# Moving residuals, turns and last convolutions of a fused four-layer kernel across its pair and layer changes

## What is computed

```python
# L0: window attention, L1: state-space mixer (x, z, B, C, dt from ssm_w_in)
h_lat = layer_norm(ALPHA * h_lat + g_m_l * y_lat, ln_mix_g[i], ln_mix_b[i])
f_lat = squared_relu_mlp(modulate(h_lat, sh_f_l, sc_f_l), ff_w1[i], ff_w2[i])
h_lat = layer_norm(ALPHA * h_lat + g_f_l * f_lat, ln_ff_g[i], ln_ff_b[i])
...
# L2: gated linear attention and Fourier mix, L3: attention; both then:
def conv_ffn(h, w_up, w_conv, b_conv, w_down):
    u = dwconv_centred(h @ w_up, w_conv, b_conv)
    g, v = jnp.split(u, 2, axis=-1)
    return (jax.nn.silu(g) * v) @ w_down
```

## Time and profile before

| what | value |
| --- | --- |
| median of 3 runs | 4105.22 us (4103.78, 4105.22, 4110.1) |
| profiled execution | 4101.45 us, span 4099.5 us |
| mean granted TensorE clock | 0.986 of full |
| TensorE busy (PE) | 3906.3 us, 95% of the span |
| DVE, ACT, POOL busy | 2190.2, 838.8, 575.1 us |

### The profile page before, as it was taken

The page is one execution under the profiler, slowest core; times in us unless marked ns, Lnnn a source line. Parts: engine busy times, 40 slices in busy tenths (PEclk is TensorE's granted clock), DMA queues, the critical chain, the costliest instruction groups (busy, mean ns, idle before and its releaser), DMA issues.

```text
span 4099.5 us, 47553 instructions
## 1 busy us (share of the span) xinstructions
PE 3906.3 (95%) x18322; PEld 2437.5 (59%) x18322; DVE 2190.2 (53%) x3633; ACT 838.8 (20%) x1655; POOL 575.1 (14%) x936
## 2 busy tenths in 40 slices
PE   7999999999999999999999998899999999999998
PEld 6677588844455555558744646645555444758863
DVE  0254532356667566444556016737788555538876
ACT  1166111100112312212101113521100012531000
POOL 1000000033313422400132002200001320000012
PEclk9999999999999999999999998999999999999999
DMA  5256011245412222312344212501112541002234
GB/s 186 92 187 207 21 52 62 83 165 173 137 63 93 79 84 85 106 59 93 124 165 144 72 41 84 182 25 62 52 62 72 173 166 55 22 22 83 92 124 158
DMA packets 209773, 410.69 MB, mean 100 GB/s; under 512 B 5922, under 2 KB 92280, under 8 KB 209424
## 3 DMA queue, kind: packets, MB, share of 16 engines
q1 hardware_dynamic: 203696, 386.94, 27.8%
q0 software_dynamic: 5856, 20.73, 1.6%
HBM read 405.49 MB, written 2.16 MB: 99 GB/s over the span
## 4 chain that ended last, share of the span: by engine, by line
PE 86%; DVE 7%; ACT 3%; DMA 2%; issue 1%; POOL 0%; DVEq 0%; ACTq 0%; SPq 0%
PE PS L1136 25%; PE PS L1254 18%; PE PS L1096 5%; PE PS L1069 3%; PE PS L1744 3%; PE PS L1047 3%; PE PS L1190 3%; PE PS L1758 3%; PE PS L1006 2%; PE PS L898 2%; PE PS L1745 1%; PE PS L1905 1%; PE PS L1915 1%; PE PS L1380 1%; PE PS L1349 1%
## 5 line engine op out<-in xcount | busy, mean ns | idle before, releaser
L1136 PE MATMUL PS<-UT,RING 128*128 128x256 f32 (+1 forms) x2432 | 640.0, 411 | 10.2 <-ACT BIG L2925 9.1
L1136 PEld LDWEIGHTS PS<-UT,RING 128*128 128x128 f32 x2432 | 461.5, 190 | 151.0 <-issue 14.2
L1136 PE MATMUL PS<-BIG,RING 128*128 128x256 f32 (+1 forms) x1824 | 487.7, 410 | 0.8 <-DVE BIG L2770 0.5
L1136 PEld LDWEIGHTS PS<-BIG,RING 128*128 128x128 f32 x1824 | 345.9, 190 | 106.5 <-DVEq L1981 1.5
L1254 PE MATMUL PS<-RING,BIG 128*128 128x512 f32 x810 | 376.7, 594 | 4.3 <-ACT GATE L2961 2.4
L3540 POOL TENSOR_TENSOR GATE<-BIG 128x128 f32<-128x128 f32 x68 | 33.8, 497 | 1707.5 <-DVE BIG L2776 583.3
L2631 DVE TENSOR_TENSOR RING<-RING 128x512 f32<-128x512 f32 x135 | 108.7, 805 | 297.9 <-DMA RING<-ff_w_dram 176.0
L1254 PEld LDWEIGHTS PS<-RING,BIG 128*128 128x128 f32 x810 | 152.0, 191 | 186.1 <-issue 181.6
L1254 PE MATMUL PS<-RING,RES_TMP 128*128 128x512 f32 x536 | 247.2, 604 | 16.1 <-DVE RING L2634 12.8
L1254 PE MATMUL PS<-RING,GATE 128*128 128x512 f32 x544 | 248.6, 600 | 9.6 <-DVE UT L2663 4.4
L1254 PEld LDWEIGHTS PS<-RING,RES_TMP 128*128 128x128 f32 x536 | 103.0, 193 | 148.3 <-issue 126.0
(11 more groups left out here) (457 smaller groups left out, 5986.1 us busy)
## 6 DMA issues: line engine op xcount, KB each, us to landing
RING<-ff_w_dram SPq DMA_DIRECT2D x112, 1024.0 KB, 5.0
RING<-w_mod_dram SPq DMA_DIRECT2D x48, 2048.0 KB, 8.1
RING<-w_ffn_down_dram SPq DMA_DIRECT2D x55, 1024.0 KB, 4.9
RING<-w_ffn_up_dram SPq DMA_DIRECT2D x44, 1024.0 KB, 5.1
RING<-ssm_w_in_dram SPq DMA_DIRECT2D x8, 2048.0 KB, 8.0
RING<-ssm_w_out_dram SPq DMA_DIRECT2D x4, 2048.0 KB, 7.8
RING<-w_even_in_dram SPq DMA_DIRECT2D x4, 2048.0 KB, 8.0
RING<-att_w_in_dram SPq DMA_DIRECT2D x3, 2048.0 KB, 11.7
```

The costliest lines, as they stand in the source:

```text
L1136: m = mm(bank(bank_, n), a[:, k, :], b[:, k, :], start=k == 0, stop=k == 3)
```

## The change

Seven edits, all of order; no arithmetic is added or dropped.

1. `combined` no longer runs `added(q, 0, 0)` between takes 1 and 2. It moves to DVE's work of slot 1 of the next pair (in L2 and L3 together with `added(q, 0, 1)`, and the others move up). Each take waits for its own product by place.
2. In the last slot of the last pair of each layer the products go in the order P1, P6, P2, P5, P3, P7, P4.
3. The half turns hooked at slots 7 to 10 (L2) and 11 to 14 (L1) of a pair move one slot earlier.
4. `mixer1`, g = 0: C's weights are loaded and used before B's, C's ring half is given back at once, and tile 5 is turned directly behind tile 4.
5. `mixer2`: the turns of tiles 2 and 3 are hooked one place earlier.
6. From L2 to L3: ACT's copy of the turned tile 5 comes only before the key/value copy of tile 2 of `mixer3`.
7. L2 and L3: the convolutions of the last two channel groups move into DVE's work of slots 2 and 4 of down; POOL sums the tokens of slots 2 to 5 before it waits for the hidden values.

```diff
-                    at = {0: 8, 1: 11, 2: 7}[L]
+                    at = {0: 8, 1: 10, 2: 6}[L]
...
+        DOWN_ORDER = ["P1", "P2", "P3", "P7", "P5", "P6", "P4"]
+        DOWN_END = ["P1", "P6", "P2", "P5", "P3", "P7", "P4"]
...
-                           {(0, 0): lambda: outputs_taken(1), (2, 0): lambda: turn_tokens(2, "m", 2), (2, 1): lambda: turn_tokens(2, "m", 3)})
+                           {(0, 0): lambda: outputs_taken(1), (1, 1): lambda: turn_tokens(2, "m", 2), (2, 0): lambda: turn_tokens(2, "m", 3)})
...
                     take(V.tensor_tensor(y1, y2, b("P2"), ALU.add))
-                    early()
-                    dve.wait_ge(S("down_products_done"), 5 * g + 5)
+                    dve.wait_ge(S("down_products_done"), 5 * g + down_place(L, q, "P6"))
                     take(V.tensor_tensor(y2, y2, b("P6"), ALU.add))
+                    dve.wait_ge(S("down_products_done"), 5 * g + down_place(L, q, "P5"))
                     take(V.tensor_tensor(y4, y2, b("P5"), ALU.add))
...
                     if L == 0:
-                        return {2: [partial(added, q, 0, 1)], 3: [partial(added, q, 1, 0)], 4: [partial(added, q, 1, 1)],
+                        return {1: [partial(added, q, 0, 0)], 2: [partial(added, q, 0, 1)], 3: [partial(added, q, 1, 0)], 4: [partial(added, q, 1, 1)],
...
+                if L >= 2:
+                    work[0, 2], work[0, 4] = [partial(last_channels, 0)], [all_channels]
...
-                    if L >= 2:
+                    if L >= 2 and p + 1 < PAIRS[L]:
                         convolved(p, 0)
-                if L < 2:
-                    return
-                convolved(PAIRS[L] - 1, 1)
-                post("hidden_ready")
-                post("conv_vectors_used")
+                return partial(convolved, PAIRS[L] - 1)
...
-                            else:
+                            elif N != 3 or t == a:
                                 turned_tokens(N, "m", t, 4 if N == 1 else 6)
...
+                    if (t, c0) == (2, 1024):
+                        turned_tokens(3, "m", 5)
...
-                        for c0, n in ((b0, 128), (b0 + 512, 128), (SSM_DI + g * 512, 512), (g * 512, 512)):
+                        for c0, n in ((b0 + 512 * (g == 0), 128), (b0 + 512 * (g > 0), 128), (SSM_DI + g * 512, 512), (g * 512, 512)):
...
                         turn_tokens(1, "m", 4, b=4)
+                        turn_tokens(1, "m", 5, b=4)
                         pe.wait_ge(S("ssm_vectors_in"), 112)
                         place(dt)
                         steps_of(0, LAT)
-                        turn_tokens(1, "m", 5, b=4)
```

More of the change, by code:

```diff
@@ L273, in down_banks, with down_order, down_place @@
                     2: dict(P1=0, P2=2, P3=3, P7=6, P5=1, P6=5, P4=4), 3: dict(P1=0, P2=1, P3=4, P7=6, P5=5, P6=3, P4=2)}[L]
+        DOWN_ORDER = ["P1", "P2", "P3", "P7", "P5", "P6", "P4"]
+        DOWN_END = ["P1", "P6", "P2", "P5", "P3", "P7", "P4"]
+        def down_order(L, q):
+            return DOWN_END if q == tiles_of(L)[0] // 2 - 1 else DOWN_ORDER
+        def down_place(L, q, name):
+            return [p for p in down_order(L, q) if p not in ("P3", "P4")].index(name) + 1
         def down_blocks(t):
@@ L1254, in product @@
                             return mm(bank(banks[name]), a, b, start=s == 0, stop=last)
-                        def done(m):
-                            if last:
-                                m.then_inc(S("down_products_done"), 1)
                         weights(t)
                         pe.wait_ge(S("down_tokens_summed"), down_tokens_summed(L, i))
-                        done(product("P1", a11, b11))
-                        done(product("P2", a12, b21))
-                        used(product("P3", s4, b22))
-                        pe.wait_ge(S("down_weights_summed"), down_weights_summed(L, i))
-                        done(product("P7", s3, t3))
-                        done(product("P5", s1, t1))
-                        done(product("P6", s2, t2))
-                        product("P4", a22, t4).then_inc(S("down_slots_done"), 1)
+                        operands = {"P1": (a11, b11), "P2": (a12, b21), "P3": (s4, b22), "P7": (s3, t3), "P5": (s1, t1), "P6": (s2, t2), "P4": (a22, t4)}
+                        summed = False
+                        for name in down_order(L, q) if last else DOWN_ORDER:
+                            if name in ("P7", "P5", "P6", "P4") and not summed:
+                                pe.wait_ge(S("down_weights_summed"), down_weights_summed(L, i))
+                                summed = True
+                            m = product(name, *operands[name])
+                            if name == "P3":
+                                used(m)
+                            elif name == "P4":
+                                m.then_inc(S("down_slots_done"), 1)
+                            elif last:
+                                m.then_inc(S("down_products_done"), 1)
                         if (q, s) in hooks:
@@ L1708, in mixer1 @@
                     else:
-                        wb = ring(weights(t0), 8, 128)
+                        xb, xc = place(cv) * 1024, place(cv) * 1024
+                        wc = ring(weights(t0), 8, 128)
+                        pe.wait_ge(S("down_products_taken"), 7 * (tiles_of(0)[0] // 2 - 1) + 1)
+                        seen(1, "m", 3)
+                        for k in range(KD):
+                            m = mm(PS[:, xc:xc + LAT], wc[:, k, :], UT[:, k, 0:LAT], start=k == 0, stop=k == KD - 1)
+                        used(m)
+                        wb = ring(weights(t0 + 1), 8, 128)
                         outputs_begun(0)
-                        xb = place(cv) * 1024
-                        seen(1, "m", 3)
                         for k in range(KD):
@@ L1715, in mixer1 @@
                         outputs_taken(0)
-                        wc = ring(weights(t0 + 1), 8, 128)
-                        x = place(cv) * 1024
-                        for k in range(KD):
-                            mm(PS[:, x:x + LAT], wc[:, k, :], UT[:, k, 0:LAT], start=k == 0, stop=k == KD - 1)
                         turn_tokens(1, "m", 4, b=4)
+                        turn_tokens(1, "m", 5, b=4)
                         pe.wait_ge(S("ssm_vectors_in"), 112)
@@ L1727, in mixer1 @@
                             mb = mm(PS[:, xb + 512:xb + 512 + CTX], wb[:, k, :], UT[:, k, LAT:TOK], start=k == 0, stop=k == KD - 1)
-                        mb.then_inc(wused, 2)
+                        used(mb)
                         start_of_steps()
@@ L2479, in mixer1 @@
                     for n in range(6):
-                        ready(cv, t0 + n if n < 2 else t0 + 2 if n == 5 else None)
+                        ready(cv, t0 + (n if g else 1) if n < 2 else t0 + 2 if n == 5 else None)
                         x = n % 4 * 1024
@@ L2648, in take, with combined @@
                     dve.wait_ge(S("down_products_taken"), taken["n"])
-                def combined(q, early):
+                def combined(q):
                     g = g0 + q
@@ L2815, in _ @@
                 residual(L, flow(L, "mixed", ntok), T0[L, "out"], n)
-                paired_up(L)
+                last_channels = paired_up(L)
                 if L == 0:
                     offer(flow(1, "conv", 4))
-                paired_down(L)
+                paired_down(L, last_channels)
                 post("layer_done")
@@ L3631, in _ @@
                 if L in next_of:
+                    ahead = 2 if L < 2 else 6
+                    sums_of_down_tokens(L, range(2, ahead))
                     pool.wait_ge(S("hidden_ready"), nth(L))
@@ L3634, in _ @@
                     behind = 14 if L < 2 else 10
-                    sums_of_down_tokens(L, range(2, behind))
+                    sums_of_down_tokens(L, range(ahead, behind))
                     store_gates(next_of[L])
```

15 lines of the change are left out of this document (10 added, 5 removed).

## The result

The changed kernel takes 4057.5 us (median of 4 runs, 4056.13 to 4061.04), the kernel before 4106.18 us on the same chip (its three runs and a fourth): ratio 0.9882, 95% interval 0.9865 to 0.9899. Its profiled execution took 4056.13 us, span 4054.1 us, 45.4 us less than before, at a mean granted clock of 0.991 (0.987 to 0.991 in its four runs). The median lies where it was forecast; in the sum behind it one term is 3.1 us too large, one is right as a whole and wrong in both its parts, and the stretches that the change doesn't touch moved by up to 1.9 us one way and 3.2 us the other.

The account below looks back on a forecast made before the run. TensorE was taken to bound the kernel, with gains only in its idles and low clock: 35.3 us idle plus 12.4 us clock, 47.7 off 4101.45, gives 4053.8; the median, 3.77 above, 4057.5 us, range 4047 to 4076.

Parts of the forecast that it names:

- The take chain: Pair changes: without the residual between takes and the turn ahead of P1's copy, 15.6 us idle and 3.6 us clock gained.
- The last convolutions: Down stage of L2 and L3: waits of 5.15 and 2.41 us go, 7.9 us with tails, plus 2.65 us clock.
- Start of L3: L3's first products: earlier start and a shorter wait behind ACT's and DVE's work, 4.8 us idle, 2.6 us clock.
- End: End of the kernel: one residual fewer between the last takes and the last norm, about 0.4 us gained.
- Start of L2: L2's start: earlier turn hides ACT's 3.04 us copy but for about 0.5; net 2.3 us idle, 1.8 us clock.
- Rival D: Pair changes: waits only change names, P3 waiting for something else that ends at the same time; 4100 to 4108 us, chance 0.02.
- Start of L1: L1's mixer: x's weights land earlier, so its products start 4.3 us sooner; 1.6 and 0.2 us of clock at x.
- Rival B: Whole kernel: clock loss moves elsewhere or stays, little of 12.4 us comes back; 4067 to 4070 us, chance 0.2.

Follow-up runs that it names:

- The control: The changed kernel, unaltered, on another chip: 4055.38 us against 4098.6 us for the kernel before there, ratio 0.9891.

## Why the prediction was right, and where it was off

- *The take chain* (15.6 us and 3.6 of clock): the six changes gained 19.2 us in the first profile (4.2 + 2.1 + 2.3 + 1.8 + 7.0 + 1.9, rounded). Undone, they cost 14.9 us with L2's turn still in its new slot. What I missed is that the same residual alone would have cost 5.2 us at L1's start; only edit 2 makes that small.
- *The last convolutions* (7.9 us and 2.65): 8.5 + 2.7 = 11.2 us, and 9.5 when undone. The cover was judged too large: "less 3.32 us of idle it makes them 1.0 us late, under the 3.75 us of slack" holds in the middle of a pair, and not at a stage's start, where 1.3 us was left. The term held because this was still above nothing.
- *Start of L3* (4.8 and 2.6 us): 7.5 measured. *End* (0.4): 0.5.
- *Start of L2* (2.3 and 1.8): 3.7 measured, and near the 4.1 forecast only by luck. "The turn one place earlier hides the second but for about 0.5" failed: 2.69 us of 3.04 stayed, so that the idle fell by 0.3 us (5.13 to 4.78) and not by 2.3. The first wait didn't grow either. The other 3.4 us are clock, 1.7 behind each of two waits of before, where I had counted one. Rival D, on one place: the wait changed its name. Whether edit 5 is worth anything is open, since no run undoes it alone.
- *Start of L1*: the term that was mis-sized as a whole. Its idle came out: 5.03 us (0.94 + 3.13 + 0.96) of the 9.16 in the trace before, 4.1 us gained for a forecast 4.3. Its clock didn't. I had the 1.8 us of low clock behind the 5.73 us wait come back, and they did. But a wait of 3.13 us took the place of the one of 3.04, and this one has low clock behind it, 0.9 us on the turn and 2.0 us on the steps, where the old one had none: 3.0 us in all, not 6.1. Rival B, on one place.
- *What no term had*: 1.1 us ahead of the first change, 0.7, 1.9 and -3.2 us in stretches that the change leaves alone, 0.5 us together. The 1.9 us are clock that the kernel before happened to lose: 0.95 of full was granted there from 3650 to 3686 us, and 1.00 in the changed kernel. In the fourteen profiles the stretch up to the linear attention's row took 470.1 to 474.7 us and the attention of L3 229.1 to 232.6.
- *The median* was hit by luck. The profiled execution took 4056.13 us where 4053.8 was forecast, 2.3 us too much; and the median lies 1.4 us above it, not 3.77 as before. The two nearly cancel. The control gave 43.2 us of gain in the median where the first chip gave 48.7.

No run settles why the clock falls behind one wait of 3 us and not behind another, or what ties the surplus of 4 and 7 us in two of the medians to their edits, if anything.

## What to carry to other kernels

Work that sits between reads which another engine waits for should move behind them, but look at once at the next reader: the same work may have been early for somebody else, and it takes a second edit to keep that. Before counting a wait as gone, ask what the awaited engine does at that time: a turn moved earlier left the wait where it was, because the copy behind it came no earlier. Measure slack at the place where it is to be spent; at the start of a stage an engine that idles later on may be running behind. And price a removed idle in two parts, the idle and the clock behind it: the first came out to some 0.2 us at nearly every place, L2's start excepted; the second can come back behind a wait that stays, as at L1's start.
